# Expert pairs across groups, their tokens gathered by transposes with completed permutations, in a four-layer hybrid decoder step

## The reference

```python
def hier_moe(u, w_rg, b_rg, w_re, b_re, w1, w3, w2):
    x = u.reshape(-1, D_MODEL)
    pg = jax.nn.softmax((x @ w_rg).astype(F32) + b_rg.astype(F32), axis=-1)
    pg_top, g_idx = lax.top_k(pg, 1)
    le = ((x @ w_re).astype(F32) + b_re.astype(F32)).reshape(-1, MOE_GROUPS, MOE_EPG)
    le_g = jnp.einsum('tge,tg->te', le, jax.nn.one_hot(g_idx[:, 0], MOE_GROUPS, dtype=F32))
    top_l, e_idx = lax.top_k(le_g, MOE_TOPK)
    wts = pg_top * jax.nn.softmax(top_l, axis=-1)
    ...
    h = jax.nn.silu(jnp.einsum('td,edf->tef', x, w1)) * jnp.einsum('td,edf->tef', x, w3)
    y = jnp.einsum('tef,efd->td', h * combine[:, :, None].astype(h.dtype), w2)
```

## Time and profile before

| | |
|---|---|
| median of the runs | 2059.68 us |
| profiled execution | 2062.35 us, span 2060.6 us |
| TensorE busy | 1978.9 us, 96% of the span |
| VectorE, ScalarE, GpSimd busy | 38%, 29%, 6% |
| moved by DMA | 629.00 MB, mean 305 GB/s |
| mean granted TensorE clock | 0.973 |

### The profile page before, as it was taken

How to read it: one execution, slowest core, us unless ns; L and a number is a source line. 1 busy time by engine, 2 the same in 40 slices (tenths; PEclk the granted TensorE clock), 3 DMA queues, 4 the chain that set the end, 5 groups by cost and what they waited for, 6 DMA issues and landing times. The chain is left out here.

```text
span 2060.6 us, 29909 instructions
## 1 busy us (share of the span) xinstructions
PE 1978.9 (96%) x11247; PEld 1283.0 (62%) x11247; DVE 773.6 (38%) x1791; ACT 595.8 (29%) x1353; POOL 119.2 (6%) x100
## 2 busy tenths in 40 slices
PE   8989999999999689899999999999999989999998
PEld 6877864444777366654545888655446877754444
DVE  4699131222112348222212363222224699231222
ACT  3486121112122117311112334211113487121111
POOL 0233000000100000000000000000000233000000
PEclk9999999999999679999999999999999999999999
DMA  9789499999738883499998464799997789499996
GB/s 328 255 269 280 126 366 422 421 421 364 250 107 270 253 251 153 175 405 421 421 421 296 143 210 169 268 422 421 422 414 232 244 283 267 142 358 422 421 422 274
DMA packets 243121, 629.00 MB, mean 305 GB/s; under 512 B 14184, under 2 KB 169112, under 8 KB 193352
## 3 DMA queue, kind: packets, MB, share of 16 engines
q1 hardware_dynamic: 229064, 611.75, 79.5%
q0 software_dynamic: 2368, 8.48, 1.3%
q10 hardware_dynamic: 11584, 7.37, 1.2%
HBM read 600.36 MB, written 35.56 MB: 309 GB/s over the span
## 5 line engine op out<-in xcount | busy, mean ns | idle before, releaser
L1561 PE MATMUL bank<-ring,e_xg 128*64 128x512 f32 x1536 | 336.7, 594 | 0.0
L696 PE MATMUL bank<-uT,ring 128*128 128x264 f32 x1280 | 298.8, 392 | 0.0
L696 PEld LDWEIGHTS bank<-uT,ring 128*128 128x128 f32 x1280 | 244.2, 193 | 48.3 <-issue 7.5
L1561 PEld LDWEIGHTS bank<-ring,e_xg 128*64 128x64 f32 x1536 | 107.5, 137 | 211.1 <-issue 202.4
L1589 PE MATMUL bank<-e_late,e_hT 128*64 128x512 f32 x1024 | 226.8, 595 | 2.7 <-ACT e_hT L1707 2.7
L1453 DVE TENSOR_TENSOR xT<-xT,bank 128x264 f32<-128x264 f32 x256 | 110.0, 430 | 225.3 <-PE bank L1612 221.8
L1445 DVE TENSOR_TENSOR e_hg<-e_sg,bank 128x512 f32<-128x512 f32 x32 | 22.0, 688 | 390.2 <-PE bank L1561 390.2
L1703 ACT ACT_TABLE_LOAD x32 | 41.1, 1283 | 435.1 <-PE bank L1561 435.1
L1589 PEld LDWEIGHTS bank<-e_late,e_hT 128*64 128x64 f32 x1024 | 70.7, 137 | 134.8 <-issue 127.9
L2915 PE MATMUL bank<-uT,ring 128*128 128x264 f32 x512 | 122.8, 401 | 2.0 <-DVE uT L405 2.0
L1537 PE MATMUL bank<-e_to_row,e_u_nat 128*128 128x128 f32 x1024 | 124.5, 275 | 0.0
(11 more groups left out here) (493 smaller groups left out, 2202.8 us busy)
## 6 DMA issues: line engine op xcount, KB each, us to landing
ring<-in_moe_w SPq DMA_DIRECT2D x192, 1024.0 KB, 10.7
e_late<-in_moe_w SPq DMA_DIRECT2D x192, 1024.0 KB, 12.5
ring<-in_m_w_in SPq DMA_DIRECT2D x40, 1024.0 KB, 9.2
s_hbuf<-in_ssm SPq DMA_DIRECT2D x32, 512.0 KB, 5.8
out_ssm_s<-s_hbuf SPq DMA_DIRECT2D x32, 512.0 KB, 3.7
ring<-in_m_w_out SPq DMA_DIRECT2D x16, 1024.0 KB, 8.0
ring<-in_h_w_in SPq DMA_DIRECT2D x16, 1024.0 KB, 5.6
n_page<-in_cache_cmp SPq DMA_DIRECT2D x48, 256.0 KB, 4.9
```

Of the source, the lines that this page charges most:

```text
L696: mm = nc.tensor.matmul(bank[p % 3][:, 0:T], W.view(s, KT, 256)[:, k, c:c + 128], uT[:, k], start=(k == 0), stop=(k == KT - 1))
L1561: mm = nc.tensor.matmul(bank[b][CAP * j:CAP * j + CAP, :], xg[:, EK // 2 * h + k, CAP * j:CAP * j + CAP], rows_of(key)[:, k], start=(h + k ...
```

## The change

Seven things. The expert pairs are (p, p+8) and no longer (2p, 2p+1), in the order of weights, rows and factors. From the second pair on the tokens are gathered by transposes, one for each tile and chunk, whose second operand is `to_row` completed to a permutation (free slots get tokens that are not taken: `free_places`); the prompt tiles 1 and 2 go to different banks (Y and X) and VectorE puts them together with two masks. Places and counts are kept in SBUF for that (`save_places`). The transposes of tile 0 (8 of the 24) move from the MoE's front to the end of the mixer. One filler matmul of 264 columns at the MoE's front gives way to two small ones that count. Filler matmuls (`keep_warm`) are put at the norms, at the mixers' starts and at the very start. The down matmuls wait for two of VectorE's steps on the banks Y.

```diff
-                        W.add_rows(up_half(I[name][layer, 2 * p + j:2 * p + j + 1], h), EK // 2, FF)
+                        W.add_rows(up_half(I[name][layer, p + NE // 2 * j:p + NE // 2 * j + 1], h), EK // 2, FF)
...  first_norm, TensorE and VectorE
+                        pe.wait_ge(*dve_done.at(1))
+                        keep_warm(uT[:, 0, 0:128], uT[:, 0], 4)
                         pe.wait_ge(*consts_in.at(1))
...
+                        keep_warm(ones, xT[:, 0], 2)
-                        pe.wait_ge(*dve_done.at(5))
+                        pe.wait_ge(*dve_done.at(6))
                         spread_quarters(rs[:]).then_inc(*pe_done.one())
...
+                        link(nc.vector.memset(uT[:, 0], 0.0))
...
+        def keep_warm(w, x, times):
+            for _ in range(times):
+                nc.tensor.matmul(bank[6][:, 0:T], w, x, start=True, stop=True)
+        def turn_last_tokens():
+            for h in range(2):
+                for k in range(4):
+                    nc.tensor.transpose(bank[2 + h][:, 128 * k:128 * k + 128], uT[:, 4 * h + k, T - 128:T], ident)
...  each mixer: at its start on TensorE, and at its end after the last sum_x
+                env["keep_warm"](ones, xT[:, 0], 1)
...
+                env["turn_last_tokens"]()
                 pe.wait_ge(*x_root.at(1))
                 env["turn_logits"](zT[:, KT])
...  moe, sum_x (the norm after the loop)
             mm.then_inc(*norm["x_norm_step"].one())
+            env["keep_warm"](ones, xT[:, 0], 2)
             pe.wait_ge(*norm["x_norm_step"].at(3))
...  moe, VectorE
+                def rows_to(p):
+                    nc.vector.tensor_tensor(to_row..., slot_no (128 numbers) ..., slot[:, :, bass.ds(p, 1)]..., ALU.is_equal).then_inc(*to_row_ready.one())
+                    for mask, k in ((from_prompt, 0), (from_last, 1)):
+                        bound = base[:, k]...
+                        nc.vector.tensor_tensor(mask[:], numbers, bound, ALU.is_ge).then_inc(*to_row_ready.one())
+                def save_places():     # 3 small operations, after pe_done.at(6)
+                def free_places(done): # 16 small operations, each waits for the one before
...
-                def fill(h, p):
-                    x = xg[:, 4 * h:4 * h + 4]
-                    nc.vector.tensor_copy(x, bank[X[h]][:].rearrange("p (k r) -> p k r", k=4)).then_inc(*xg_copied.one())
+                def fill(p):
+                    dve.wait_ge(*to_row_ready.now())
+                    for h in range(2):
+                        dve.wait_ge(*gathered.of(p, 2, 3 + h))
+                        nc.vector.tensor_tensor(xg[:, 4 * h:4 * h + 4], bank[Y[h]][:]..., spread(from_prompt), ALU.mult) \
+                            .then_inc(*xg_copied.one())
+                    for h in range(2):
+                        dve.wait_ge(*xg_copied.now())
+                        nc.vector.tensor_copy(v[:, 0, 7:8], v[:, 0, 5:6])
+                        nc.vector.copy_predicated(xg[:, 4 * h:4 * h + 4], spread(from_last), bank[X[h]][:]...) \
+                            .then_inc(*xg_copied.one())
+                        dve.wait_ge(*xg_copied.now())
+                        add_decode(h, p + 1)
...
                     combine(comb_done)
+                    free_places(comb_done)
...
                 mark["crowded"] = dve_done.now()
+                save_places()
...  moe, TensorE
-                for t, h in halves:
+                for t, h in halves[2:]:
...
-                keep_on(range(0, 1))
+                nc.tensor.matmul(bank[1][:, 0:2 * NE], ones, at[:, 0:2 * NE], start=True, stop=False, skip_group_check=True)
+                nc.tensor.matmul(bank[1][:, NE:2 * NE], ones, at[:, 0:NE], start=False, stop=True, skip_group_check=True).then_inc(*pe_done.one())
...
+                def gather(h):
+                    for t, b in ((1, Y[h]), (2, X[h])):
+                        for c in range(4):
+                            mm = nc.tensor.transpose(bank[b][:, PAIR * c:PAIR * c + PAIR], u_nat[:, t, 4 * h + c], to_row[:, t].rearrange("p e r -> p (e r)"))
+                    mm.then_inc(*gathered.one())
...  moe, TensorE, down matmuls
                     for f in range(2):
                         for c in range(2):
+                            if f == 0 and not last:
+                                pe.wait_ge(*xg_copied.of(p, 4, 3 + c))
                             down(f, c)
...  moe, ScalarE: the copies of tile 0 no longer wait for TensorE
```

More of the change, by code:

```diff
@@ L1206, in moe @@
     PAIR = 2 * CAP
+    PAIRS = NE // 2
     with ExitStack() as st:
@@ L1394, in _ @@
                 mark["exponents"] = dve_done.now()
[L1396 removed]
+                dve.wait_ge(*pe_done.at(5))
                 link(nc.vector.scalar_tensor_tensor(out=row[:], in0=taken[:, 0:TT].rearrange("p t e -> p (t e)"), scalar=-float(UNTAKEN),
                                                     in1=bank[0][:, 0:TT * NE], op0=ALU.mult, op1=ALU.add))
[L1399 to L1403 removed]
+                first, second = slice(0, PAIRS), slice(PAIRS, NE)
@@ new lines, in free_places @@
+                def free_places(done):
+                    link = linker(dve, done)
+                    link(TTn(pos[:], pos[:], base[:, 0:2], ALU.subtract))
+                    link(TTn(held[:], base[:, 1:3], base[:, 0:2], ALU.subtract))
+                    link(TTn(spot[:], pos[:, :, first], pos[:, :, second], ALU.add))
+                    link(nc.vector.tensor_scalar(spot[:], spot[:], -1.0, cst("token_no"), ALU.mult, ALU.add))
+                    link(TTn(jump[:], spot[:], base[:, 0:2, first], ALU.is_ge))
+                    link(TTn(jump[:], jump[:], held[:, :, first], ALU.mult))
+                    link(TTn(bound[:], base[:, 0:2, second], held[:, :, first], ALU.subtract))
+                    link(nc.vector.scalar_tensor_tensor(out=bound[:], in0=spot[:], scalar=-float(CAP), in1=bound[:], op0=ALU.add, op1=ALU.is_ge))
+                    link(TTn(bound[:], bound[:], held[:, :, second], ALU.mult))
+                    link(TTn(spot[:], spot[:], jump[:], ALU.add))
+                    link(TTn(spot[:], spot[:], bound[:], ALU.add))
+                    link(TTn(jump[:], taken[:, 1:TT, first], taken[:, 1:TT, second], ALU.add))
+                    link(nc.vector.scalar_tensor_tensor(out=spot[:], in0=jump[:], scalar=2.0 * UNTAKEN, in1=spot[:], op0=ALU.mult, op1=ALU.add))
+                    link(nc.vector.scalar_tensor_tensor(out=slot[:], in0=rows[:, :, second], scalar=float(CAP), in1=rows[:, :, first], op0=ALU.add, op1=ALU.min))
+                    link(TTn(slot[:, 1:TT], slot[:, 1:TT], spot[:], ALU.min))
+                    link(TTn(weight[:], comb[:, :, first], comb[:, :, second], ALU.add))
@@ L1447, in pair @@
                     if not last:
-                        for h in range(2):
-                            dve.wait_ge(*gathered.of(p, 2, 3 + h))
-                            fill(h, p + 1)
+                        fill(p)
                     for c in range(KT):
@@ L1519, in _ @@
                     mm.then_inc(*pe_done.one())
-                def keep_on(chunks):
-                    for k in chunks:
-                        nc.tensor.matmul(bank[1][:, 0:T], ones, uT[:, k], start=True, stop=True)
                 pe.wait_ge(*mark["taken"])
@@ L1616, in gathered_program @@
                     pe.wait_ge(*act_done.at(7))
-                    gather(0)
-                    gather(1)
+                    gather_first(0)
+                    gather_first(1)
                     with pe.Fori(0, PAIRS - 1) as p, ExitStack() as turn:
```

72 lines of the change are left out of this document (51 added, 21 removed).

## The result

The changed kernel takes 2046.07 us (median of 4 runs, 2044.84 to 2049.09), the kernel before 2060.23 on the same chip: ratio 0.9935, 95% interval 0.9918 to 0.9952, so 14 us faster. I had forecast 2028.7, 31 faster, with a range down from 2043. The direction was right, the size not, and the time lies outside the range. One execution of run 10's kernel was in a slow state (3997 us) and is left out of its time and ratio.

What follows compares the result with a forecast made beforehand. TensorE was taken to bound the kernel, with transfers close behind and next to bind. 28.6 + 0.4 - 1.5 + 3.0 + 1.5 - 1.0 = 31.0 us off the profiled 2062.35 gave 2031.4, median 2028.7, range 2016 to 2043.

Steps and rivals of the forecast that it cites:

- 28.6 us from the loops: MoE loops: each ends earlier by its last load's lead only, 28.8 us in sum, 28.6 with four short wake-ups.
- The gathers: MoE turns from the second pair: transposes replace float32 matmuls, 0.90 us a half, 1.79 us saved a turn, 50.1 in all.
- The transfers are late next: MoE loops: TensorE's turn 27.4 us, the transfers' 29.9; the lead is gone at the sixth or seventh pair.
- Mixer starts also get loads that now queue behind what the MoE left ... -1 us (0 to -6): Mixer starts: the first six loads land 15 us after the last w2, near or just after entry; 1 us lost.
- This is again lead, not time: MoE fronts: 1.5 us of TensorE saved by eight fewer transposes gives only lead, except +0.4 us for layers 1 and 2.
- Early turns, -1.5: Before the MoE: eight transposes ahead of `turn_logits` make four entries 0.38 us later each; 1.5 us lost, bounds 0 and -3.5.
- The fillers, +3.0 and +1.5: Filler matmuls hold the clock up: 3.0 us gained at layer 2's mixer, 1.5 us at the very start.
- the gain is given back: Rival: mixers wait for first loads or states, or the clock drops in last turns; 2042 us, chance 9%.
- TensorE alone as the bound: Rival: TensorE alone bounds, so all 50.1 us and the 2.4 of the rest are gained; 2007 us, chance 7%.
- No clock fell in the gathers: Rival judged: transposes count as rest and TensorE runs at 1.2 GHz for a stretch each turn; 2102 us, chance 4%.
- The order (p, p+8): Rival: the new order of experts slows the transfers, at 5% giving 2073 us; chance 4%.

Runs made afterwards that it cites:

- run 10: Changed kernel plus three matmuls without use in the MoE's front, six loads still sent ahead: 2039.15 us, ratio 0.9894.
- Run 1: Changed kernel with two instead of six of the next mixer's loads sent ahead after the MoEs of layers 1 and 2: 2035.13 us, ratio 0.9885.
- 2: Changed kernel without any filler matmul, six loads sent ahead: 2046.0 us, ratio 0.9938.
- 9: Changed kernel with two loads sent ahead and without the filler matmuls: 2041.24 us, ratio 0.9908.
- 3: Changed kernel with all 24 transposes back in the MoE's front, none early: 2043.4 us, ratio 0.991.
- 5: Kernel before, with ten instead of twelve loads a turn (second half of w2 loaded once a layer and reused): 2056.67 us, ratio 0.9985.
- 6: Kernel before, with two instead of six of the next mixer's loads sent ahead: 2059.72 us, ratio 0.9993.
- 8: Changed kernel with two loads sent ahead and all 24 transposes in the front: 2032.1 us, ratio 0.9864.
- run 7: Changed kernel with two loads sent ahead and three matmuls without use in the MoE's front: 2029.43 us, ratio 0.9851.
- 12: Changed kernel with two loads sent ahead, three matmuls without use in the front and all 24 transposes there: 2029.85 us, ratio 0.9848.
- run 4: Changed kernel with ten instead of twelve loads a turn (second half of w2 loaded once a layer and reused): 2011.28 us, ratio 0.9767.

## Why the prediction was wrong, step by step

For the profiled executions I had 28.6 us from the loops, 0.4 from the fronts and 2.0 from all the rest (-1.5 + 3.0 + 1.5 - 1.0). They gave 27.1, -2.6 and -9.0. The loops were right; the rest had the wrong sign.

- **The gathers**: right. 0.87 us a half against 0.90, a turn of 27.36 against 27.4, and the masked copy of 512 columns 0.725 us against "at most twice 0.69"; no wait for VectorE ahead of the down matmuls in the body of the loop.
- **The transfers are late next**: right in place and size. Turns of 27.36 us up to the fifth, 27.4 to 28.7 for the sixth, 29.8 to 29.9 for the seventh; the loops gave 27.1 us where 28.6 were expected. TensorE's waits for weights are 3.8 + 11.5 + 2.3 = 17.6 us, 4.4 a layer. The Trainium skill ("DMA: Bandwidth & Descriptors", "Where 436 GB/s comes from") would have had a limit of about 358 GB/s for a core's loads from HBM; these turns ran at 421.
- **"Mixer starts also get loads that now queue behind what the MoE left ... -1 us (0 to -6)"**: the step that failed most, with 8.6 us lost in the mixers. I looked at the loads' own lateness, and they were not late. What was late is what shares the way with them: TensorE's next instructions. Two branches of 4.40 and 4.15 us against 1.36 and 0.88, and the low clock behind them. Run 1 puts the whole at 11 us, of which the traces place 8.5: 5.8 idle and 2.7 at the low clock. It was in the trace: the fetch was in 1.1 us before the last matmul ahead of the branch ended, and I moved TensorE 7 us against the transfers without asking for whom this was near. That it hit two branches and spared layer 0's is not something that I can derive.
- **"This is again lead, not time", +0.4 for the fronts**: failed. A front is covered up to 11.8 us (layer 0), and one of 13.1 costs about 1.6 us, since the first slots are freed by the first gate matmuls and the transfers stand still until then (16 GB/s in 878:880). The fronts of layers 1 and 2 rose to 14.3 and 12.8: TensorE, rid of eight transposes, waits 2.20 us for VectorE's pairing, and low clock follows. In one trace this could be chance, as the kernel before has it in layer 1; over the runs it is not: the four fronts add up to 47.6 to 49.1 us in the four with early turns and no matmuls in the front (the changed kernel, 1, 2, 9), and to 43.6 to 46.5 in the five with all 24 transposes there (the kernel before, 3, 5, 6, 8). Three matmuls without use, in this kernel, are worth 6 to 8 us by the medians and ratios. In the profiled executions run 7 is 2.7 us shorter than run 1, with 3.4 between entry and end of the four MoEs; run 1's profiled execution lies 3.5 us below its median, so these two don't contradict the medians.
- **Early turns, -1.5**: not told from nothing. Runs 8 and 12 differ from 1 and 7 by -3.0 and +0.4 us.
- **The fillers, +3.0 and +1.5**: 4.7 in run 9, by an uncertainty as large. In the changed kernel the late branch stood behind them with a longer gap than they fill. Layer 2's mixer was at the low clock for half as long as before (1107.7 to 1111.1), but so it was in runs 2 and 9 without fillers. The first ring matmuls of the start came 1.55 us sooner (14.49 against 16.04), and 150 us later nothing was left of it; in runs 3, 4, 10 and 12, with the same fillers, they came at 16.7 to 17.4, later than without. So the +1.5 isn't shown either.
- **The rivals.** Of them "the gain is given back", with 2042, was nearest in result and had low clock and mixers in it. TensorE alone as the bound, 2007, is what run 4 shows once two loads of twelve are gone (2011). No clock fell in the gathers: 1.00 in the turns. The order (p, p+8) left the landings at 2.49 us.

With both faults mended the kernel takes 2029.4 us, 17 below the changed one. That this lies near the forecast's 2028.7 is in part luck: the forecast counted 4.5 us for fillers that no run shows, and the front's matmuls also take away low stretches that the kernel before has.

What stays open: why the fetch got behind the second landing in two layers and not in layer 0, and how far that is the loads and how far the place of the code, since run 2 changed it as well; what makes the clock fall after 0.92 us of waiting in one layer and not in another; the stretches at the low clock between 600 and 780 us, in layer 1's mixer, which move from run to run without an edit near them; and whether the front's matmuls would help the kernel before, whose fronts have low stretches too, which wasn't run.

## What to carry to other kernels

When an edit moves one engine against the transfers, list everything that shares the DMA at the points that come earlier, instruction fetches at block borders included, and ask which had under a move's length to spare. Keep loads for the next stage to what its first matmuls need: here two of 1 MiB; six cost about 10 us, none 11. An engine that becomes faster ahead of a wait gives the time to the wait, and on TensorE sometimes the clock as well; a few matmuls without use are a cheap test for that. And read a difference between two traces from the point that the edit touches: here 5 us of 15 lay ahead of it.

## What the runs showed of the hardware

- With loads of 1 MiB filling the queue, a fetch of 16 KB of TensorE's instructions started at a load's landing: at the second after the loop's end behind the MoEs of layers 2 and 1 (1545.84 after 1545.67; 1104.47 after 1104.30), with a branch of 4.15 and 4.40 us, and at the first behind layer 0's (504.13 and 504.15), with 1.03. In the kernel before and in runs 1 and 7 (two loads ahead) it started 1.2 to 1.9 us after the loop's end, and the branches were 0.6 to 1.6 us.
- With 12 transfers of 1 MiB a turn the rate stayed at 421 GB/s and 2.49 us a landing while TensorE's turns shortened by 6%. At the branch into layer 3's mixer, with that mixer's loads under way, it was 348 to 354 GB/s, and they landed 2.7 to 3.0 us apart.
- After a gap of 2.20 us TensorE ran at 0.58 of full clock (3.40 us for 16 records of 128 columns instead of 2.05); with the same gap cut to 0.43, 1.00. After gaps of 0.92 us in one run the 16 records took 3.54 us in layer 0 and 2.05 in layer 3.
- A masked copy takes 725 ns for 512 columns, 437 for 256, a product of 512 columns out of PSUM 691.
